# Decode keys scored by TensorE from cache pages laid out by head dimension, in a hybrid decoder step on one core

## The reference

```python
past_k = cache_sb_k[layer][page_table].reshape(DEC_BATCH, n_pages * PAGE_SIZE, H_SB, HEAD_DIM)
past_v = cache_sb_v[layer][page_table].reshape(DEC_BATCH, n_pages * PAGE_SIZE, H_SB, HEAD_DIM)
z = jnp.einsum('bqhd,bkhd->bhqk', q, k).astype(jnp.float32) / math.sqrt(HEAD_DIM)
z = z + bias
log_rest = jnp.where(earlier, jax.nn.log_sigmoid(-z), 0.0)
log_stick = lax.cumsum(log_rest, axis=3, reverse=True) - log_rest
a = jnp.where(earlier, jnp.exp(jax.nn.log_sigmoid(z) + log_stick), 0.0)
out = jnp.einsum('bhqk,bkhd->bqhd', a, v)
```

## Time and profile before

| | |
|---|---|
| median of 3 runs | 1296.95 us (1292.42 to 1301.7) |
| profiled execution | 1296.18 us, of which the span of the trace is 1294.5 us |
| PE, DVE, POOL, ACT busy | 71%, 60%, 33%, 28% of the span |
| DMA | 481.11 MB, mean 372 GB/s |

### The profile page before, as it was taken

One profiled execution on the slowest core, in us unless ns is written; L12 is line 12 of the kernel. 1 busy time (PEld: TensorE's weight loads), 2 busy tenths in 40 slices (PEclk: granted clock), 3 DMA queues, 4 the chain that ended last, 5 costly groups with the idle time before them and its releaser, 6 DMA issues.

```text
span 1294.5 us, 13955 instructions
## 1 busy us (share of the span) xinstructions
PE 923.2 (71%) x3176; PEld 424.4 (33%) x3176; DVE 776.0 (60%) x1690; ACT 358.8 (28%) x969; POOL 424.5 (33%) x451
## 2 busy tenths in 40 slices
PE   3999602646465658979978877778767787777874
PEld 1454202334111213468623333323323333332321
DVE  3112799987333322443277777777787777777755
ACT  0020102323111002012333233333244433444323
POOL 1002100010133220001165455554545555544551
PEclk9999856576677768989999999999989999999997
DMA  9999978999888786999999999999989999999996
GB/s 367 421 386 368 354 246 285 362 355 339 287 275 281 251 253 229 325 378 391 395 417 423 427 428 428 427 428 427 428 369 418 428 427 428 427 428 428 427 427 279
DMA packets 87798, 481.11 MB, mean 372 GB/s; under 512 B 11881, under 2 KB 12234, under 8 KB 46418
## 3 DMA queue, kind: packets, MB, share of 16 engines
q0 software_dynamic: 52096, 349.25, 66.4%
q1 hardware_dynamic: 35666, 131.44, 28.3%
HBM read 477.40 MB, written 70.32 MB: 423 GB/s over the span
## 4 chain that ended last, share of the span: by engine, by line
DMA 47%; PE 21%; issue 12%; DVE 8%; ACT 5%; SPq 2%; POOL 2%; POOLq 2%; DVEq 0%; ACTq 0%
DMA R<-in_uv,idst 28%; PE ps L887 8%; DMA R<-in_sb_k 6%; DMA R<-in_sb_v 5%; DMA out_dil_v_s<-in_dil_v 5%; PE ps L838 5%; DVE R L1259 3%; PE ps L793 2%; PE ps L661 2%; DMA const<-in_consts 2%; POOL R L472 1%; ACT wgt L1131 1%; SPq L285 1%; POOLq L285 1%; DMA R<-in_uv,idec 1%
## 5 line engine op out<-in xcount | busy, mean ns | idle before, releaser
L887 PE MATMUL ps<-R,diag 128*128 128x512 f32 x1024 | 490.9, 630 | 139.9 <-ACT diag L1150 139.9
L472 POOL DMA_INDIRECT R<-in_uv,idst x256 | 323.5, 1264 | 325.1 <-PE ps L887 248.7
L1592 DVE CUSTOM_DVE_ANT_0 R<-R,H 128x1024 f32<-128x1024 f32 x264 | 319.2, 1223 | 171.8 <-DMA R<-in_uv,idst 162.1
L887 PEld LDWEIGHTS ps<-R,diag 128*128 128x128 f32 x1024 | 196.6, 200 | 434.3 <-ACT diag L1150 222.9
L398 POOL DMA_DIRECT2D R<-in_wts x44 | 23.5, 534 | 373.3 <-PE ps L506 166.9
L1128 ACT ACTIVATE gel<-dots 128x2 f32<-128x2 f32 x132 | 26.8, 203 | 374.6 <-DVE dots L1592 374.6
L1259 DVE TENSOR_TENSOR R<-R 128x1024 f32<-128x1024 f32 x64 | 78.0, 1218 | 84.7 <-ACT R L943 46.1
L661 PE MATMUL ps<-R,ast 128*32 128x512 f32 x256 | 72.6, 853 | 72.6 <-DMA R<-in_sb_v 70.9
L1150 ACT ACTIVATE diag<-const,wgt 128x128 f32<-128x128 f32 x256 | 88.9, 394 | 13.7 <-PE ps L887 0.7
L567 PE MATMUL ps<-R,HT 128*128 128x512 f32 x192 | 85.5, 598 | 1.5 <-DMA R<-in_wts 1.5
L1261 DVE TENSOR_REDUCE Z<-R 128x1024 f32 x64 | 78.1, 1220 | 9.1 <-DVE R L1259 0.2
(11 more groups left out here) (262 smaller groups left out, 884.0 us busy)
## 6 DMA issues: line engine op xcount, KB each, us to landing
R<-in_wts POOLq DMA_DIRECT2D x48, 1024.0 KB, 11.2
R<-in_sb_k SPq DMA_DIRECT2D x128, 256.0 KB, 5.4
out_dil_k_s<-in_dil_k SPq DMA_DIRECT2D x32, 1023.5 KB, 8.6
out_dil_v_s<-in_dil_v SPq DMA_DIRECT2D x32, 1023.5 KB, 8.7
R<-in_sb_v SPq DMA_DIRECT2D x64, 256.0 KB, 4.0
R<-in_sb_v POOLq DMA_DIRECT2D x64, 256.0 KB, 4.0
R<-in_uv,idst POOLq DMA_INDIRECT x256, 11.8
m_all<-in_dil_k POOLq DMA_DIRECT2D x16, 192.0 KB, 5.8
```

Of the source, the lines that this page charges most:

```text
L472: pool.indirect_dma_start(out=R[:, row_slot(k), :], out_offset=None, in_=A["uv"], in_offset=bass.IndirectOffsetOnAxis(ap=idst[:, par, k:k ...
L887: last = pe.matmul(ps[:, banks + q, :], diag[:, k % 4, :], R[:, row_slot(k), D + q * 512:D + (q + 1) * 512], start=False, stop=False, skip ...
L1592: dve.tensor_tensor_reduce(u, u, H[:, t, :], 1.0, 0.0, ALU.mult, ALU.add, dots[:, k:k + 1]).then_inc(s["dot_done"], 1)
```

## The change

- Key pages are laid out on the host as (head dimension of a head pair) x (4 head pairs x 128 positions): partition p of a page holds dimension p % 64 of heads 2c + p // 64. Size and transfer size per partition (2 KB) stay.
- The sample queries are turned once (`turn_group`) and copied by DVE into a zeroed tile `qz` (8 copies), so that one matmul of 32 columns gives the logits of one head pair for both pages of a chunk. `keys(b)` runs 32 matmuls of 256 columns per sequence, four column groups side by side, and accumulates all sequences in banks 6 and 7. DVE's `page_scores` and the spread queries go.
- After the last sequence DVE scales and adds the bias (2 operations), PE turns the banks (8 transposes), DVE copies them out (16 operations). Softplus, suffix sums and exp of the page weights move from behind the pairs into pairs 0 and 1.
- The ring has eight slots (a whole sequence), in `R[:, 4..5]` and `R[:, 8..9]`; SP loads the even chunks and POOL the odd ones, for keys as for values. Value pages of sequence 0 are requested as the last keys are used. Window values get six slots, and sequences 2 to 5 are requested as the last value slots come free.
- Rotary goes from POOL to DVE. The window copies are spread differently: 16 pieces after the first key pages as before, 8 (was 16, among key and value pages) beside the stick-breaking pairs, and 40 (was 32) after the window values.
- The stick-breaking pairs are written out instead of looped.

```diff
-KVS = 4
+KVS = 8
-        KV = [Rf[:, WSLOTS * 2048 + s * 1024:WSLOTS * 2048 + (s + 1) * 1024].rearrange("p (g n) -> p g n", g=KVP)
-              for s in range(KVS)]
+        KV = [Rf[:, at * 1024:(at + 1) * 1024].rearrange("p (g n) -> p g n", g=KVP) for at in (8, 9, 10, 11, 16, 17, 18, 19)]
...
+        def key_pages(eng, b, chunks, first=False):
+            for c in chunks:
+                page_chunk(eng, b, c, A["sb_k"], kv_ready, [] if first else [(s["k_used"], b * CPB + (c - CPB + 1))])
+        def value_pages(eng, b, chunks, first=False):
+            for c in chunks:
+                page_chunk(eng, b, c, A["sb_v"], kv_ready,
+                           [(s["k_used"], (NB - 1) * CPB + c + 1)] if first else [(s["v_used"], b * CPB + (c - CPB + 1))])
...
+            sp.wait_ge(s["w_used"], 4)
+            key_pages(sp, 0, EVEN, first=True)
+            for odd in range(2):
+                copy_windows(0, odd)
+            with sp.Fori(1, NB) as b:
+                key_pages(sp, b, EVEN)
...
+            value_pages(sp, 0, EVEN, first=True)
+            copy_windows(1, 0)
+            with sp.Fori(1, NB) as b:
+                value_pages(sp, b, EVEN)
...
+            weight_rounds(2, 4)
+            weight(4, 0)
+            weight(4, 1)
+            for b in range(1, NB):
+                key_pages(pool, b, ODD)
+                if b < NB - 1:
+                    weight((b + 17) // WSLOTS, (b + 17) % WSLOTS)
...
+            def keys(b):
+                for cc in range(CPB):
+                    half, bank, at = cc // 4, 6 + cc % 4 // 2, cc % 2 * WC
+                    pe.wait_ge(kv_ready[cc], b * 32 + 32)
+                    for c in range(QUADS):
+                        last = pe.matmul(ps[c * QUAD:(c + 1) * QUAD, bank, at:at + WC], qz[:, half, c, b, :],
+                                         KV[cc][:, :, c * P:(c + 1) * P], start=(b == 0 and half == 0),
+                                         stop=(b == NB - 1 and half == 1), skip_group_check=True)
+                    last.then_inc(s["k_used"], 1)
...
+                    elif r > 0:
+                        if (r, k) == (1, 1):
+                            pe.wait_ge(s["qz_ready"], 1)
+                        keys((r - 1) * WSLOTS + k - 1)
+            keys(NB - 1)
+            pe.wait_ge(s["zs_ev"], 1)
+            for n in range(NPG // 2):
+                last = pe.transpose(ps[:, 6 + n // 4, n % 4 * P:(n % 4 + 1) * P], zl[:, n * P:(n + 1) * P], ident)
+            last.then_inc(s["zT_mm"], 1)
...
-            with dve.Fori(0, NB // 2) as b:
-                page_scores(b, range(CPB))
...
-                page_scores(g + 4, (0, 1))
```

More of the change, by code:

```diff
@@ L437, in _, with windows_and_values @@
             weight_rounds(9, 10)
-            def odd_value_pages(b, first=False):
-                for c in range(1, CPB, 2):
-                    page_chunk(pool, b, c, A["sb_v"], v_ready,
-                               [] if first and c < KVS else [(s["v_used"], b * CPB + (c - KVS + 1))])
-            def windows_and_values(i, first=False):
+            def windows_and_values(i):
                 for j in range(2):
@@ L613, in sticks_pair @@
                 last.then_inc(s["sc_mm"], 1)
-                if not first:
+                if first:
+                    pe.wait_ge(s["z_l"], 1)
+                else:
                     pe.wait_ge(s["ada_ev"], g + 2)
@@ L635, in sticks_pair @@
                 last.then_inc(s["o_mm"], 1)
-            sticks_pair(0, first=True)
-            with pe.Fori(1, NH // 2) as g:
-                sticks_pair(g)
+            for g in range(NH // 2):
+                sticks_pair(g, first=(g == 0))
+                if g == 0:
+                    pe.wait_ge(s["z_suf"], 1)
+                    for half in range(2):
+                        c = slice(half * 512, (half + 1) * 512)
+                        pe.matmul(ps[:, 3 + half, :], tri, zl[:, c], start=True, stop=False)
+                        last = pe.matmul(ps[:, 3 + half, :], ones, zt[:, c], start=False, stop=True)
+                    last.then_inc(s["z_s"], 1)
             def add_rows(base, j, first, rows):
@@ L709, in _ @@
             dilated_turn(0)
-            pe.wait_ge(s["z_suf"], 1)
             pe.wait_ge(s["qd_ev"], NB)
-            for half in range(2):
-                c = slice(half * 512, (half + 1) * 512)
-                pe.matmul(ps[:, 3 + half, :], tri, zl[:, c], start=True, stop=False)
-                last = pe.matmul(ps[:, 3 + half, :], ones, zt[:, c], start=False, stop=True)
-            last.then_inc(s["z_s"], 1)
             dilated_values(0, first=True)
@@ L1264, in _ @@
-            with dve.Fori(0, NB // 2) as b:
-                page_scores(b, range(CPB))
+            dve.wait_ge(s["qz_mm"], 1)
+            for half in range(2):
+                for j in range(2):
+                    f = slice(j * HD, (j + 1) * HD)
+                    for b in range(2):
+                        last = dve.tensor_copy(
+                            qz_flat[f, half, bass.ds(b, 2, step=2), bass.ds(half * 2 * NB + j * NB, NB, step=QUAD + 1)],
+                            ps[f, 5, b * P:b * P + 2 * QUAD].rearrange("p (k n) -> p k n", k=2)[:, :, 0:NB])
@@ new lines, in _ @@
+            dve.wait_ge(s["k_used"], NB * CPB)
+            for half in range(2):
+                last = dve.tensor_scalar(zl[:, half * 512:(half + 1) * 512], ps[:, 6 + half, :], SCALE, bias_row, ALU.mult, ALU.add)
+            last.then_inc(s["zs_ev"], 1)
+            dve.wait_ge(s["zT_mm"], 1)
+            for n in range(NPG // 2):
+                for half in range(2):
+                    page = n + half * (NPG // 2)
+                    last = dve.tensor_copy(
+                        z1[:, page * PAIRS:(page + 1) * PAIRS].rearrange("p (c n) -> p c n", c=4),
+                        ps[:, 6 + n // 4, n % 4 * P:(n % 4 + 1) * P].rearrange("p (c n) -> p c n", c=4)[:, :, half * 16:half * 16 + 16])
@@ L1267, in both @@
+            last.then_inc(s["z_l"], 1)
             def both(a):
```

266 lines of the change are left out of this document (114 added, 152 removed).

## The result

The changed kernel takes **1253.55 us** (median of 4 runs, 1252.19 to 1258.98), the kernel before 1294.68: ratio 0.9687, 95% interval 0.963 to 0.9744. The profiled execution has a span of 1250.9 us against 1294.5.

A forecast was written before the change was run, and what follows sets the result against it. Time was taken as DMA work plus DMA idle time, the work unchanged. Idle of 0.9 + 5 + 26 + 4 + 9.1 + 2.8 + 10.7 = 58.5 us against 68.2 gave 1286 us, range 1263 to 1308.

The forecast's parts named there:

- Rates: DMA speeds per busy time: weights and copies mixed 398 GB/s, pages and window rows 320 GB/s.
- The ledger of idle: DMA idle time, (1 - share) x length, summed over all stages: 68.2 us before, 58.5 us after.
- the stage of dependencies: Logits, pairs and dilated setup, after the last key: 113 us long with 87 us of DMA work, 26 us new idle.
- Key stage: From 94 us to the last key: 125 us of DMA work plus 5 us idle, ending at about 224 us.
- Value stage: From 337 us: 33.3 MB at 320 GB/s, 104 us, plus 4 us idle, ending near 445 us.
- The spill: After the values: some 8 of 40 window copies run into the expert stage and lengthen it by what they weigh.
- Pages are held back by the ring, not by packet size: Key and value stages: pages could move at 423 GB/s, together 42 us less, 1244 us; chance 0.06.
- The value stage keeps its pace: Value stage: PE's order keeps it at 18.8 us per sequence, 27 us idle instead of 4, 1309 us; chance 0.10.
- PE's clock falls in the key stage: Key stage: slots of 25 us instead of 15.7 for some six, 35 us more idle, 1321 us; chance 0.07.
- The idle time only moves: Stage after the keys: pairs at half clock, 122 us, idle 35 us, 1295 us in all; chance 0.22.
- PE at full clock through the pairs: Stage after the keys: 104 instead of 113 us, idle 17 us, 1277 us in all; chance 0.20.
- the last one: Key scoring: column groups don't run side by side, `keys(b)` takes 17 us, over 1330 us in all; chance 0.03.

The follow-up runs named there:

- experiment 8: The changed kernel with the last 8 window copies left out, so those output rows are not written: 1229.56 us.
- experiment 1: The changed kernel with value pages requested only four chunks ahead, keys still eight: 1288.53 us.
- experiment 7: The changed kernel with 8, 12 or 16 more window copies requested beside the stick-breaking pairs, as many fewer behind the values: 1234.63, 1247.64 and 1250.4 us.
- experiments 1 to 3: The changed kernel with pages requested only four chunks ahead: values alone 1288.53 us, keys alone 1288.05 us, both 1324.92 us.
- the ring alone: The kernel before with only the ring changed to eight slots and window values loaded behind the value pages; VectorE still scores keys: 1241.19 us.

## Why the prediction was wrong

**The view of the bound held**: time is DMA work plus DMA idle, and a late copy is paid for (24 us for eight, experiment 8).

**The step that failed is the one under "Rates"**: "Pages and window rows (2 KB a partition), nearly alone in the value stage: 266 / 0.83 = 320 GB/s". It took busy share times length for work, as if a busy engine always moved bytes at its speed. Pages moved at over 400 GB/s with eight chunks requested, at 272 with four (experiment 1). From it came the sentence "The change moves the same bytes in transfers of the same shape, so its whole gain has to come out of those 68 us". The gain had a second source, the 30 us of busy time computed above. The ledger of idle was near in its sum, 55.6 us measured against 58.5 forecast, but partly by errors that cancel; stage by stage 12.8 (5 forecast), 27.3 (26), 0 (4), 2.6 (9.1 + 2.8, since values end earlier and only one gap stays), 1.5 (0), tail 10.5 (10.7).

**By landmarks** the 33 us between 1286 and 1253 are: keys end at 221.4 us (224 forecast), 3 us; the stage of dependencies 108 us (113), 5; values 98 us, 329.2 to 426.7 (108, 337 to 445), 10; from there to the first gather on the chain 143 (145), 2; from it to the end 681.5 (694.8), 13. This last stretch was never added up by itself: it grew by 22 us over the 659.9 before (from the gather at 634.6 us), about what eight copies weigh, while the 35 of the forecast were only what the ledger, with its dear pages, left over.

- *Key stage.* The sum of 125 us of work was 10 too long, the idle of 5 was 8 too short (PE's slots stop a full ring). The errors nearly cancel, so the landmark was right for a wrong reason.
- *Stage of dependencies.* Pairs follow each other in 18.4 and 17.1 us (17.9 forecast), the stage's share is 0.75. "26 us of new DMA idle time" was right (27.3), and experiment 7 shows what could be had from it: eight copies placed there bring 19 us.
- *Value stage.* POOL's rate, 1.23 us per page, bounds it: 8 pages and window rows 12 us a sequence. Measured 98 us for the eight; POOL issues back to back, and the first pages of two sequences stand 12.9 us apart, where SP pauses in every sequence:

```profile
349.08 0.58 POOL L286 DMA_DIRECT2D R<-in_sb_v  x1 [0.84 <-issue]
...
361.99 0.58 POOL L286 DMA_DIRECT2D R<-in_sb_v  x1 [0.84 <-issue]
```

  I had that bound and put 15 us of DMA above it.
- *The spill.* It came (copies issued until 593.2 us, the first gather on the chain at 569.4).

**The rivals.** "Pages are held back by the ring, not by packet size" was given 0.06 and 1244 us; it is what happened, at 1253.6, by experiments 1 to 3. (Its 10 us too many are about the idle that the key stage has above the 5 forecast, 8.) What stood against it, "320 to 360 GB/s of busy time in every stage that holds pages", was no evidence: all these stages had the same ring of four. The right reading of the earlier trace rows was that nothing in it varied the depth, and then both values deserved weight. The rule of the Trainium skill quoted there ("DMA: Bandwidth & Descriptors", "Specifications": line rate from 512 bytes on) nearly agrees with the packet records: 84 ns in the middle for 2 KB, 159 for 4 KB and 309 for the gathers' 8 KB are 390, 412 and 424 GB/s for 16 engines. So the size of the packets counts for 8%, and not for the quarter between 320 and 423. (Nor were all pages in 2 KB packets: GpSimd's half of the value pages went in 4 KB before the change too.) The Trainium skill also warns of the step itself: "Perfetto Trace Analysis", section "Identifying the Most-Contended Engine", calls the occupancy of DMA misleading, since there are 16 engines, and asks for bytes against the peak instead. That 0.83 busy went with 266 GB/s and 1.00 with 364 bears out the advice, though for another reason.

"The value stage keeps its pace" fell: the ring set it, not PE's order. "PE's clock falls in the key stage" fell: 0.82, and slots of at most 9.2 us. "The idle time only moves" fell: its 122 us of pairs and 35 of idle were 108 and 27.3. "PE at full clock through the pairs" (104 us) came half-way, at a granted clock of 0.78. `keys(b)` in 3.64 us rules out the last one. Of the signs, the stage of 108 us, the share of 0.75 in it and the share of 1.00 with the values came; DMA at 0.95 in the key stage did not (0.90), and pages above 360 GB/s were named as a sign of being wrong.

**Left open.** The kernel before with the ring and with its window copies placed anew wasn't tried. The fastest complete version is the full change with 8 more copies beside the pairs, 1234.63 us; whether it is faster than the ring alone (1241.19) is open, as said in experiment 7. Why 34 us of depth in the key stage come out above the 21 to 30 expected was not taken apart further, and neither was the way in which the short ring makes packets slow.

## What to carry to other kernels

Before calling a stage DMA-bound, divide its bytes by its length and compare with the best stage of the same trace; here a busy share of 0.83 at 266 GB/s with the values, beside a stage at 1.00 and 423, went with too few transfers under way, and a deeper ring or a second issuer, alone, is a cheap thing to try first. Count what one engine can issue: size of a transfer over the time between issues. And when a big rewrite carries a small change of buffers with it, price the small change by itself first: here it was at least the whole gain. Last, where a rewrite also moves background work, compare versions that have equally much of it late: 12 us that looked like the price of the rewrite went with eight late copies.

## What the runs showed that I had not expected

- The trace's DMA share can be high at a low rate: page streams with one issuer show 0.7 at 200 to 245 GB/s, with a ring of four 0.83 at 266, with eight 1.00 at 364 (up to 421 in single slices).
- A 256 KB page with its page number read from a table takes SyncE 1.24 us and GpSimd 1.14 us to issue, of which the DMA instructions themselves are 0.34 and 0.54 us. One engine so feeds 211 to 230 GB/s (262 KB over the period); two together would feed 441 by the same reckoning, an estimate, and 421 was seen.
- A page lands in 3.1 to 3.8 us in the middle with one issuer, and in 5.6 to 7.5 us when two engines keep eight chunks of values going. At the least it took 2.4 us from SyncE and 2.9 from GpSimd, both among the value pages of the kernel before. The Trainium skill, "DMA: Bandwidth & Descriptors", section "Anatomy of one DMA — SWDGE (gpsimd) path", fits 2.0 us plus bytes over 436 GB/s for DMAs of GpSimd, which gives an estimate of 2.6 us for a page; GpSimd's shortest landing lies 0.3 us above it.
- GpSimd sends such a page in 64 packets of 4 KB, SyncE in 128 of 2 KB (and 16 of 4 bytes each). Per byte the larger ones are 5% shorter in the middle (159 ns against 2 x 84), for 64 pages an estimated 2 us: too little to be seen in a time.
- Copies beside dependent work are free only up to a point: 8 copies of 1 MB more gained 19 us, and with 12 PE waited for a weight chunk for 10.20 us at once.
